# Two of nine expert tiles as dense products over all experts, with the trunk's work set 1.6 times as dense per gather slot

## The reference

```python
def block(xb):                                   # 128 tokens
    q = jnp.einsum('td,dc->tc', xb, wq).reshape(-1, PEER_HEADS, 2, PEER_DK // 2)
    s = jnp.einsum('thpd,hpnd->thpn', q, keys)   # 2 x 128 keys per head
    sv, si = lax.top_k(s, PEER_TOPK)
    cand = (sv[:, :, 0, :, None] + sv[:, :, 1, None, :]).reshape(-1, PEER_HEADS, kk)
    cidx = (si[:, :, 0, :, None] * N_KEYS + si[:, :, 1, None, :]).reshape(-1, PEER_HEADS, kk)
    top_s, pos = lax.top_k(cand, PEER_TOPK)
    eidx = jnp.take_along_axis(cidx, pos, axis=-1)
    w = jax.nn.softmax(top_s, axis=-1)
    hid = jnp.einsum('td,thkd->thk', xb, u[eidx])
    act = jax.nn.gelu(hid, approximate=False) * w
    return jnp.einsum('thk,thkd->td', act, v[eidx])
...
y = rmsnorm(h + PEER(rmsnorm(h)))
```

## Time and profile before

| what | value |
|---|---|
| median of three runs | 4519.91 us (4505.94 to 4530.8) |
| span of the profiled execution, first to last instruction | 4507.1 us |
| around that span, against the median | 12.8 us |
| PE busy | 3549.1 us, 79% |
| DVE busy | 2706.5 us, 60% |
| ACT busy | 2290.9 us, 51% |
| gathers (L1999) | 1088 |
| moved by DMA | 1390.03 MB, 1143.02 of them by the gathers' queue |

### The profile page before, as it was taken

How to read it: one execution, slowest core, us unless ns; L and a number is a source line. 1 busy time by engine, 2 the same in 40 slices (tenths; PEclk the granted TensorE clock), 3 DMA queues, 4 the chain that set the end, 5 groups by cost and what they waited for, 6 DMA issues and landing times.

```text
span 4507.1 us, 52945 instructions
## 1 busy us (share of the span) xinstructions
PE 3549.1 (79%) x18525; PEld 2675.1 (59%) x18525; DVE 2706.5 (60%) x5686; ACT 2290.9 (51%) x4217; POOL 1427.9 (32%) x1160
## 2 busy tenths in 40 slices
PE   6999799997778998777777767798878667667666
PEld 5666576575666666655555555566666445555555
DVE  3555435226789775634764588698542766756754
ACT  3222111114766464754555566656474666666675
POOL 0000000002334233324544334333332445545554
PEclk9999899998989999887888888999989776666666
DMA  2000222247999899989999999999999999999997
GB/s 80 29 29 29 89 88 76 92 131 288 352 369 387 339 373 344 417 342 366 372 352 378 348 402 332 380 412 388 366 416 323 394 415 421 421 421 421 421 418 317
DMA packets 293635, 1390.03 MB, mean 308 GB/s; under 512 B 35111, under 2 KB 100327, under 8 KB 153093
## 3 DMA queue, kind: packets, MB, share of 16 engines
q0 software_dynamic: 158720, 1143.02, 63.2%
q1 hardware_dynamic: 134669, 243.89, 15.5%
HBM read 1353.22 MB, written 33.95 MB: 308 GB/s over the span
## 4 chain that ended last, share of the span: by engine, by line
PE 37%; DMA 24%; DVE 13%; ACT 9%; issue 4%; POOL 1%; SPq 1%; ACTq 0%; DVEq 0%; POOLq 0%
DMA p_ring<-in_peer_uv,p_idx 11%; PE psum L2020 8%; PE psum L1349 7%; DMA group<-in_peer_uv,p_idx 5%; DVE p_ring L2089 4%; PE psum L1428 4%; DMA t_w<-in_w_query 4%; PE psum L1353 3%; PE psum L1394 2%; PE psum L969 2%; ACT p_ring L2055 2%; DVE group L2089 1%; PE psum L1879 1%; DVE group L1581 1%; DMA group<-in_x_all 1%
## 5 line engine op out<-in xcount | busy, mean ns | idle before, releaser
L1999 POOL DMA_INDIRECT p_ring<-in_peer_uv,p_idx x806 | 986.1, 1223 | 1389.1 <-PE psum L2020 1217.8
L2020 PE MATMUL psum<-ident,p_ring 128*128 128x128 f32 x5944 | 1005.6, 326 | 526.9 <-ACT p_ring L2055 526.7
L2089 DVE CUSTOM_DVE_ANT_0 p_ring<-p_ring,p_xn 128x1024 f32<-128x1024 f32 x806 | 979.1, 1219 | 522.9 <-DMA p_ring<-in_peer_uv,p_idx 522.5
L2020 PEld LDWEIGHTS psum<-ident,p_ring 128*128 128x128 f32 x5944 | 834.1, 169 | 725.6 <-ACT p_ring L2055 664.0
L2055 ACT ACTIVATE p_ring<-p_ring,p_act_w 128x1024 f32<-128x1024 f32 x743 | 853.6, 1149 | 24.3
L2049 ACT ACTIVATE p_gl<-p_hid 128x1 f32<-128x1 f32 x1088 | 216.7, 199 | 988.8 <-DVE p_hid L2089 986.7
L1999 POOL DMA_INDIRECT group<-in_peer_uv,p_idx x282 | 366.2, 1298 | 1007.1 <-issue 550.4
L2020 PE MATMUL psum<-ident,group 128*128 128x128 f32 x2112 | 371.0, 335 | 179.1 <-ACT group L2055 178.8
L2089 DVE CUSTOM_DVE_ANT_0 group<-group,p_xn 128x1024 f32<-128x1024 f32 x282 | 342.9, 1219 | 203.5 <-DMA group<-in_peer_uv,p_idx 201.1
L2020 PEld LDWEIGHTS psum<-ident,group 128*128 128x128 f32 x2112 | 306.9, 174 | 250.5 <-ACT group L2055 231.8
L1349 PE MATMUL psum<-group,t_w 128*128 128x384 f32 (+1 forms) x1344 | 445.0, 475 | 3.7 <-DMA t_w<-in_w_merge 1.9
(11 more groups left out here) (332 smaller groups left out, 4550.2 us busy)
## 6 DMA issues: line engine op xcount, KB each, us to landing
t_w<-in_w_merge SPq DMA_DIRECT2D x72, 768.0 KB, 8.2
t_w<-in_w_query SPq DMA_DIRECT2D x48, 576.0 KB, 7.6
group<-in_cache_kT SPq DMA_DIRECT2D x64, 256.0 KB, 7.7
group<-in_cache_v SPq DMA_DIRECT2D x64, 256.0 KB, 3.4
p_ring<-in_peer_uv,p_idx POOLq DMA_INDIRECT x806, 10.7
t_w<-in_w_conv SPq DMA_DIRECT2D x24, 512.0 KB, 7.6
t_w<-in_w_outs SPq DMA_DIRECT2D x24, 512.0 KB, 7.9
t_w<-in_w_fox SPq DMA_DIRECT2D x24, 512.0 KB, 21.3
```

The source lines that it names most:

```text
L1999: pool.indirect_dma_start(row[g], None, io["peer_uv"], bass.IndirectOffsetOnAxis(ap=idx[:, u, c:c + 1], axis=0)).then_inc(row_loaded[g], 16)
L2020: last = pe.matmul(acc[u][:, k * P:(k + 1) * P], row[given[at][0]][:, D + k * P:D + (k + 1) * P], ident[:, :], start=(c == 0 and k % 4 == ...
L2089: dve.tensor_tensor_reduce(out=row[g][:, 0:D], in0=row[g][:, 0:D], in1=xn[:, u, :], scale=1.0, scalar=0.0, op0=ALU.mult, op1=ALU.add, accu ...
```

## The change

Tiles 4 and 5 leave the slots (`ORDER`); 832 slots remain. For their 256 tokens all 16384 experts are computed, in 128 blocks of 128 experts (block j holds the experts whose second key is j; partition p the first key). Their choices still run, but end in first keys, second keys and weights, which go to scratch memory. From slot 456 a matrix of weights is built: for four tokens at a time DVE makes one-hot rows of the first keys and of the second keys times the weight, PE multiplies them, ACT copies the result, and SP stores it (16.8 MB) and reads it back in chunks of four blocks. From slot 496 on a block comes every 2.6 slots: the products with the block's `u` (8 matmuls of 256 columns), gelu on ACT, the product with the weights on DVE, and for every four blocks the products with `v` (16 matmuls of 512 columns, four behind each block), which DVE sums. The tables are streamed by SP, 1.05 MB a block.

The trunk's ticks are set against slots at 8 to 5, so that its 707 ticks end at slot 442. The times of the choices are written out in `WHEN`. The three extra places of the late slots are dropped, the other two end earlier (slots 199 and 260), and DVE sums rows only up to slot 65.

```diff
+ORDER = (0, 1, 2, 3, 6, 7, 8)
+DENSE = (4, 5)
...
+RATE = (8, 5)
...
+def tick(at):
+    return at * RATE[0] // RATE[1]
...
+def ticks(at):
+    return range(tick(at - 1) + 1 if at else 0, tick(at) + 1)
...
+WHEN = {1: (26, 118), 2: (146, 246), 3: (276, 318), 4: (328, 372), 5: (402, 436), 6: (448, 506), 7: (534, 630), 8: (662, 758)}
+WINDOW = {1: 0, 2: 1, 3: 2, 4: 2, 5: 3, 6: 3, 7: 4, 8: 5}
+BUILD = 456
+BLOCKS = 128
+GROUPS = ND // 4
+STORE = 32
+BUILT = BUILD + GROUPS // 2 + 4
+LOOP = BUILT + 4
+STEP = (13, 5)
+CHUNK = 4
+U_RING, V_RING, ACT_RING = 7, 7, 8
+END = max(LOOP + STEP[0] * BLOCKS // STEP[1] + 40, SLOTS + 40)
+MORE = ((0, slot_of(SAMPLE + 8)), (slot_of(PLAN1.end + 8), slot_of(FOX2.start - 12)))
...
-    return at % 2 == 0 and (20 <= at < FOX1.end + 4 or FOX2.start + 4 <= at < 4 * EXPERTS - 2)
+    return at % 2 == 0 and 20 <= at < slot_of(FOX1.end + 4)
...
+        def block_at(j):
+            return LOOP + j * STEP[0] // STEP[1]
...
+        def dense_w(sp):
+            for c in range(BLOCKS // CHUNK):
+                yield BUILT if c < 2 else block_at(CHUNK * (c - 1)) + 1
+                if c >= 2:
+                    sp.wait_ge(prod_ok, after(CHUNK * (c - 1)))
+                sp.dma_start(w_d[c % 2], io["w_scratch"][:, :, STORE * CHUNK * c:STORE * CHUNK * (c + 1)].rearrange("b p n -> p b n")).then_inc(w_loaded_d[c % 2], 16)
+        def dense_u(sp):
+            for j in range(BLOCKS):
+                yield BUILT if j < U_RING else block_at(j - U_RING) + 1
+                if j >= U_RING:
+                    sp.wait_ge(bank_ps, after(GROUPS + j - U_RING + 1))
+                sp.dma_start(u_d[j % U_RING], io["peer_dense"][j * P:(j + 1) * P, 0:D]).then_inc(u_loaded[j // CHUNK % 2], 16)
+        def dense_v(sp):
+            for j in range(BLOCKS):
+                yield BUILT if j < V_RING else block_at(CHUNK * ((j - V_RING) // CHUNK) + 2 * CHUNK - 1) + 2
+                if j >= V_RING:
+                    sp.wait_ge(out_ps, after(2 * len(DENSE) * ((j - V_RING) // CHUNK + 1)))
+                sp.dma_start(v_d[j % V_RING], io["peer_dense"][j * P:(j + 1) * P, D:2 * D]).then_inc(v_loaded_d[j // CHUNK % 2], 16)
...
+        def dense_dve(dve):
+            for n in range(GROUPS):
+                yield BUILD + n // 2 + 2
+                if n == 0:
...
+                dve.wait_ge(xt_ok, after(9 + n // 32 + 1))
+                if n >= 2:
+                    dve.wait_ge(bank_ps, after(n - 1))
+                dve.tensor_tensor(first_d[n % 2], lanes_d.unsqueeze(1).broadcast_to([P, 4, P]),
+                                  turned_d[:, 0, 4 * n:4 * n + 4].unsqueeze(2).broadcast_to([P, 4, P]), ALU.is_equal)
+                for x in range(4):
+                    last = dve.tensor_scalar(second_d[n % 2][:, x, :], lanes_d, turned_d[:, 1, 4 * n + x:4 * n + x + 1], turned_d[:, 2, 4 * n + x:4 * n + x + 1],
+                                             ALU.is_equal, ALU.mult)
+                last.then_inc(ones_ok, 1)
+            def product(j):
+                c, jj = divmod(j, CHUNK)
+                to = act_d[j % ACT_RING].rearrange("p (b t) -> p b t", t=STORE)
+                dve.wait_ge(bank_ok, after(GROUPS + j + 1))
+                dve.wait_ge(w_loaded_d[c % 2], 16 * (c // 2 + 1))
+                dve.tensor_tensor(to, to, w_d[c % 2][:, :, STORE * jj:STORE * (jj + 1)], ALU.mult).then_inc(prod_ok, 1)
+            def total(k):
+                a, hf = divmod(k % (2 * len(DENSE)), 2)
+                to = sum_d[:, a, 512 * hf:512 * (hf + 1)]
+                if k == 0:
+                    dve.wait_ge(dense_loaded, 16 * (3 + len(DENSE)))
+                dve.wait_ge(out_ps, after(k + 1))
+                if k >= 2 * len(DENSE):
+                    dve.wait_ge(add_ok, after(k - 2 * len(DENSE) + 1))
+                dve.tensor_tensor(to, to, pb[2 + k % 2], ALU.add).then_inc(add_ok, 1)
+            for c in range(BLOCKS // CHUNK + 1):
+                for x in range(CHUNK):
+                    j = CHUNK * c + x
+                    if j < BLOCKS:
+                        yield block_at(j) + 1
+                        product(j)
+                    if c:
+                        for k in range(2 * len(DENSE) * x // CHUNK, 2 * len(DENSE) * (x + 1) // CHUNK):
+                            yield block_at(j) + 2
+                            total(2 * len(DENSE) * (c - 1) + k)
...
+        def dense_act(act):
...
+            for n in range(GROUPS):
+                yield BUILD + n // 2 + 3
...
+                act.wait_ge(bank_ps, after(n + 1))
+                if n % 8 == 0 and n >= 16:
+                    act.wait_ge(wd_stored[n // 8 % 2], after(16 * (n // 16)))
+                at = 4 * n % STORE
+                act.activation(stage_d[n // 8 % 2][:, :, at:at + 4].rearrange("p j t -> p t j"), pb[n % 2].rearrange("p (t j) -> p t j", t=4),
+                               ACT.Copy).then_inc(bank_ok, 1)
+            for j in range(BLOCKS):
+                yield block_at(j) + 1
+                act.wait_ge(bank_ps, after(GROUPS + j + 1))
+                if j >= ACT_RING:
+                    act.wait_ge(out_ps, after(2 * len(DENSE) * ((j - ACT_RING) // CHUNK + 1)))
+                act.activation(act_d[j % ACT_RING], pb[j % 2][:, 0:ND], ACT.Gelu).then_inc(bank_ok, 1)
...
+        def dense_pe(pe):
...
+            for n in range(GROUPS):
+                yield BUILD + n // 2 + 3
+                pe.wait_ge(ones_ok, after(n + 1))
+                if n >= 2:
+                    pe.wait_ge(bank_ok, after(n - 1))
+                for x in range(4):
+                    last = pe.matmul(pb[n % 2][:, P * x:P * (x + 1)], first_d[n % 2][:, x, :], second_d[n % 2][:, x, :], start=True, stop=True)
+                last.then_inc(bank_ps, 1)
+            for c in range(BLOCKS // CHUNK + 1):
+                for x in range(CHUNK):
+                    j = CHUNK * c + x
+                    if j < BLOCKS:
+                        yield block_at(j)
+                        if x == 0:
+                            pe.wait_ge(u_loaded[c % 2], 16 * CHUNK * (c // 2 + 1))
+                        if j == 0:
+                            pe.wait_ge(dense_loaded, 48)
+                            pe.wait_ge(bank_ok, after(GROUPS))
+                        pe.wait_ge(bank_ok, after(GROUPS + j - 1))
+                        for k in range(KD):
+                            last = pe.matmul(pb[j % 2][:, 0:ND], u_d[j % U_RING][:, k * P:(k + 1) * P], x_d[:, k, :], start=(k == 0), stop=(k == KD - 1))
+                        last.then_inc(bank_ps, 1)
+                    if c == 0:
+                        continue
+                    for k in range(2 * len(DENSE) * x // CHUNK, 2 * len(DENSE) * (x + 1) // CHUNK):
+                        yield block_at(j) + 1
+                        a, hf = divmod(k, 2)
+                        n = 2 * len(DENSE) * (c - 1) + k
+                        if k == 0:
+                            pe.wait_ge(prod_ok, after(CHUNK * c))
+                            pe.wait_ge(v_loaded_d[(c - 1) % 2], 16 * CHUNK * ((c - 1) // 2 + 1))
+                        if n >= 2:
+                            pe.wait_ge(add_ok, after(n - 1))
+                        for y in range(CHUNK):
+                            jv = CHUNK * (c - 1) + y
+                            last = pe.matmul(pb[2 + n % 2], act_d[jv % ACT_RING][:, a * P:(a + 1) * P], v_d[jv % V_RING][:, 512 * hf:512 * (hf + 1)],
+                                             start=(y == 0), stop=(y == CHUNK - 1))
+                        last.then_inc(out_ps, 1)
...
-                    for x in ends + trunk:
+                    for due in ticks(at):
+                        for x in trunk:
+                            x.to(due)
+                    for x in work:
                         x.to(at)
```

More of the change, by code:

```diff
@@ L1656, in part_of, with kept_before @@
         def part_of(t, half):
-            return half if t == 0 else t + 1
+            return half if t == 0 else CHOSEN.index(t) + 2
+        def kept_before(t):
+            return sum(x in DENSE for x in CHOSEN[:CHOSEN.index(t)])
         def step_of(t, half):
@@ L1803, in sample_sp @@
                     sp.wait_ge(s_ps, after(32))
+                    sp.wait_ge(xt_stored, after(16 * sum(t < 6 for t in DENSE)))
                 else:
@@ L1979, in _ @@
                 pool.wait_ge(xn_stored[j], after(16))
-            work = Pace(sample_pool(pool))
-            for t, u, n, slots in tiles():
+            trunk = Pace(sample_pool(pool))
+            for q, t, u, n, slots in tiles():
                 if t == 8:
```

339 lines of the change are left out of this document (233 added, 106 removed).

## The result

The changed kernel takes 5232.32 us (median of four runs, 5214.94 to 5251.58), beside 4512.92 us (4501.03 to 4530.8) for the kernel before on the same chips: a ratio of 1.1585, 95% interval 1.1537 to 1.1632. The direction was forecast, the size was not: 4720 us with a range to 4930.

A forecast was written before the change was run, and what follows sets the result against it. The prediction took DMA time for gathers to bound the kernel before. Head 1069, trunk 1920, slots 442 to 495 230, dense stage 1460 and tail 40 summed to 4719 us of span; it said 4720, range 4420 to 4930.

The forecast's parts named there:

- What bounds the kernel before: Kernel before: DMA for gathers is the bound, at 0.93 to 1.00 beside the trunk and 1.01 in slots 707 to 1087.
- The trunk: Slots 0 to 441, the 707 trunk ticks: 1920 us (1720 to 2140), against 2441 before.
- that 84%: Five trunk stretches without units: PE's busy share rises from 75% to 84% as waits for gathers go, giving 1360 us.
- The rival in which the trunk does not become denser: Trunk: latencies set the pace, PE keeps 79.5%, DMA falls to 0.77; trunk 2140 us, whole 4939; chance 0.10.
- The build: Slots 442 to 495, choices end and weight matrix is built: DVE's work sets 230 us (190 to 270).
- The dense stage: Slots 496 to 831, 128 blocks: a round trip makes cycles of 8.64 and 12.5 us; 1460 us (1220 to 1650).
- the wait for `v`: Dense stage: the last of each four output tables lands late, stalling PE some 3 us in two of five cases, 38 us.
- the rival with the lower clock: Dense stage: PE's gaps leave a granted clock of 0.8, 13.1 us a block, 1680 us; whole 4940; chance 0.10.
- The stage's other bound: Dense stage: DMA time for 336 gathers, tables and weights, 1219 us.
- The clock: Dense stage: granted clock taken as 0.97; by the skill's rule on transposes alone 265 us more, 4984 in the sum.
- Head, tail and ring: To the first dot 1069 us; after the last slot 40 us (25 to 60); six ring places cost nothing.
- The rival in which everything overlaps: Whole kernel: PE and DMA both stay busy; trunk 1750, build 200, dense stage DMA-bound at 1260, whole 4309; chance 0.20.

The follow-up runs named there:

- e12: The kernel before, with PE adding every gathered row one slot later: 4470.83 us against 4502.28, ratio 0.993.
- e14: Changed kernel with PE adding gathered rows one slot later, and seven of each eight transposes left out in slots 66 to 440: 4703.8 us.
- e8: Changed kernel with PE adding gathered rows one slot later, and two more ring places lent in slots 269 to 439: 4753.5 us.
- e2: Changed kernel with DVE summing a dense-stage output product one slot later, behind the next dot: 5009.3 us.

## Why the prediction was wrong

The span is 515 us above the sum: 253 in the trunk, 154 in the build, 113 in the dense stage, and 5 less in head and tail together.

**What bounds the kernel before** held as far as e12 shows. **The trunk** failed at the step "Part of that idle time was waiting for gathers, and goes", which raised PE's share in five stretches from 75% to 84%; the prediction had named that 84% as the step most likely to fail. Without any gather traffic 84 us went, not the 220 that separate 2140 from 1920. PE's waits stood ahead of transposes, for a scaling that was late without gathers as well; as I read the order, its dot stood on DVE behind trunk work that waited for PE, and 1.6 ticks a slot put more of such work between two dots. The rival in which the trunk does not become denser came true by its numbers: PE was busy 81% of 2173 us, against its 79.5% and 2140, and DMA's share was 0.79 where it had 0.77. Its reason was a small part only: PE waited 35 us for query weights and 22 for attention's pieces, beside 338 for scaling. Of the 253 us that the term missed by, the later transposes return 103, most of it in slots 267 to 324. A second part is the sample's stage. The five stretches of the earlier trace rows that are not units were forecast at 1360 of their 1761 us, which would make 354 of its 458; it took 422, and between 386 and 444 in every other kernel of the table. Why it keeps that time is open, as said above. What holds the other six stretches after the later transposes is open too. Of their 1662 us gathers are worth 91, the transposes' work 66, more ring places nothing where they were lent; a slot also puts its dot on DVE and its gelu and scaling on ACT into the chains, which I did not try apart.

**The build** failed at its first sum: "DVE needs 231 us where DMA would need 138" adds up DVE's compares, dots and choices and says nothing of the loop that joins them, though the next paragraphs draw such a loop for the dense stage. With the loop opened the sum is right (243 for 230); with the loop in place it is 384.

**The dense stage** was right in its mechanism: cycles of 8.64 and 12.5 us were forecast in two and three fifths of the blocks, and the trace has 51 short ones (median 8.64 us) and 76 long ones (14.2); the wait for `v` is 28 us where 38 was forecast; PE is at 82%, DVE waits for PE's output products and PE for scaling, and the edit that opens the loop brings it to DMA's bound. It was mis-sized by 113 us: the first block waits 25 us for its table (not in the sum), and of the long cycles 55 have 13 us and more where 12.5 was forecast. The part of the sum that was too small is what follows PE's wait: over 77 waits of 2.7 to 3.5 us, the transposes and the 16 records of products behind one take 5.7 us on average, and 4.5 at the least. A clock of 0.97 was taken, 0.93 came; that is a part of the rival with the lower clock, which had 0.8. Two small terms were not worked out as stated: 553 ns for 384 columns scale to 0.74 us for the output sum and not 0.69 (the sum then measured 0.69), and nothing shows how a clock of 0.97 makes 1460 of 1402 and 38. The stage's other bound was mis-sized too: worked out at the rate of gathers alone it was 1219 us, but at a DMA share of 0.98 this mixture of gathers and tables moves 379 to 382 GB/s and takes 1335.

**The clock.** The Trainium skill (TensorE: Matmul & The Clock Gate, Part 4: PE-mode transpose) says that transposes do not count as PE-busy in the same way. The trace does not bear out that this sets the time here: in the dense stage eight transposes between products take 1.04 us as long as PE has not waited, and in e14, with most transposes gone, the trunk's granted clock fell from 0.89 to 0.81.

**Head, tail and ring** were right within 10 us; the ring's price of nothing was borne out where e8 lent places, in slots 269 to 439. **The rival in which everything overlaps** is what the dense stage becomes once PE adds rows a slot later (1335 for its 1260), but it needs that edit or that of e2.

With the later transposes the change still loses: the trunk falls by 371 us against before (2441 to 2070), but slots 442 to 495 cost 242 and the dense stage 1335 where slots 707 to 1087 cost 975, which is 602 us more and 231 net. Part of the freed DMA time went to the tables, and PE got 999 us of products (307, 219 and 472 in the page's groups).

## What to carry to other kernels

Where engines work their queues in order, draw the loop from one engine's output back to its own next input for every stage, the small ones too, before adding up busy times: in the build and the dense stage the larger of the two set the time. A step that consumes another engine's result can go one iteration later in its queue (here 9% for one step, and 0.7% in a kernel at 95% of DMA). And an idle share next to a full resource is that resource's doing only if taking the resource away moves it.
